# Token columns spread into rows: transposes of a repeated column in place of products with a unit or triangular matrix

## The reference, cut to what matters

```python
def rms_norm(x, g):
    xf = x.astype(F32)
    y = xf * lax.rsqrt(jnp.mean(xf * xf, axis=-1, keepdims=True) + EPS)
    return (y * g.astype(F32)).astype(x.dtype)
...
    # gated_delta_rule
    gc = jnp.cumsum(_chunk_gate(g), axis=-1)
    bc = _chunk_gate(beta)
    decay = jnp.exp(jnp.where(incl, gc[..., :, None] - gc[..., None, :], -jnp.inf))
...
    # mlstm_chunkwise, step
        d_log = jnp.where(incl, b_i[..., :, None] - b_i[..., None, :] + i_i[..., None, :], -jnp.inf)
        m_inter = b_i + m[..., None]
        m_t = jnp.maximum(m_inter, jnp.max(d_log, axis=-1))
        s = jnp.einsum('bhcd,bhsd->bhcs', q_i, k_i) * jnp.exp(d_log - m_t[..., None])
        den = w_inter * jnp.einsum('bhcd,bhd->bhc', q_i, n_bar) + jnp.sum(s, axis=-1)
        h = num / jnp.maximum(jnp.abs(den), jnp.exp(-m_t))[..., None]
```

## Time and profile before

| | |
|---|---|
| median of 3 runs | 2105.59 us (2104.49 to 2108.33) |
| the profiled execution | 2102.33 us, its span 2100.5 us |
| TensorE busy | 1995.4 us (95%), stationary loads 1251.3 us (60%) |
| VectorE, ScalarE, GpSimd busy | 716.2, 543.8, 120.3 us |
| the chain that ended last | PE 75%, DMA 19%, DVE 3% |
| mean granted TensorE clock | 0.978 |

### The profile page before, as it was taken

One profiled execution on the slowest core, in us unless ns is written; L12 is line 12 of the kernel. 1 busy time (PEld: TensorE's weight loads), 2 busy tenths in 40 slices (PEclk: granted clock), 3 DMA queues, 4 the chain that ended last, 5 costly groups with the idle time before them and its releaser, 6 DMA issues.

```text
span 2100.5 us, 22631 instructions
## 1 busy us (share of the span) xinstructions
PE 1995.4 (95%) x9262; PEld 1251.3 (60%) x9262; DVE 716.2 (34%) x1025; ACT 543.8 (26%) x831; POOL 120.3 (6%) x127
## 2 busy tenths in 40 slices
PE   8999999989898998989899899999999999999998
PEld 6868843333233333333233388898878888887886
DVE  6747321101010010101010275733568544335324
ACT  5246310001010100000010255234444333234125
POOL 3431000000000000000000000141000000000000
PEclk9998999999999999999999999999999999999999
DMA  9421799999999999999999822111113222223231
GB/s 266 142 71 48 298 354 425 427 427 427 428 428 429 429 428 428 428 428 429 429 427 427 339 109 81 61 41 41 61 58 140 83 94 87 84 115 110 100 141 61
DMA packets 48742, 516.27 MB, mean 246 GB/s; under 512 B 5904, under 2 KB 6032, under 8 KB 13088
## 3 DMA queue, kind: packets, MB, share of 16 engines
q1 hardware_dynamic: 46496, 508.39, 59.5%
q0 software_dynamic: 2176, 6.88, 1.5%
HBM read 508.92 MB, written 6.29 MB: 245 GB/s over the span
## 4 chain that ended last, share of the span: by engine, by line
PE 75%; DMA 19%; DVE 3%; ACT 1%; issue 1%; SPq 0%; POOL 0%; DVEq 0%; ACTq 0%
DMA arena<-in_w_gu_dram 19%; PE bank L2422 15%; PE bank L2447 5%; PE bank L912 4%; PE bank L910 4%; PE bank L911 4%; PE bank L576 3%; PE bank L578 3%; PE bank L577 3%; PE bank L2385 3%; PE bank L942 2%; PE bank L943 2%; PE bank L944 2%; PE bank L2050 2%; PE bank L2056 2%; PE bank L2052 2%
## 5 line engine op out<-in xcount | busy, mean ns | idle before, releaser
L2422 PE MATMUL bank<-arena 128*64 128x512 f32 x2048 | 480.6, 625 | 70.9 <-DMA arena<-in_w_gu_dram 67.0
L2422 PEld LDWEIGHTS bank<-arena 128*64 128x64 f32 x2048 | 162.4, 143 | 364.2 <-issue 357.6
L2917 DVE TENSOR_TENSOR arena<-arena,bank 128x256 f32<-128x256 f32 x64 | 26.9, 421 | 643.0 <-ACT arena L3158 643.0
L2447 PE MATMUL bank<-arena 128*64 128x512 f32 x1024 | 232.5, 595 | 0.6 <-ACT arena L3162 0.6
L3158 ACT ACTIVATE arena<-bank 128x256 f32<-128x256 f32 x64 | 24.6, 384 | 539.5 <-PE bank L2422 539.5
L2447 PEld LDWEIGHTS bank<-arena 128*64 128x64 f32 x1024 | 73.5, 137 | 139.4 <-issue 139.4
L910 PE MATMUL bank<-input_rounded,weight_rest 128*128 128x512 f32 x352 | 137.1, 390 | 0.0
L912 PE MATMUL bank<-input_rounded,weight_rounded 128*128 128x512 f32 x352 | 136.9, 389 | 0.0
L911 PE MATMUL bank<-input_rest,weight_rounded 128*128 128x512 f32 x352 | 136.9, 389 | 0.0
L576 PE MATMUL bank<-input_rounded,weight_rest 128*128 128x512 f32 x312 | 126.0, 404 | 0.0
L578 PE MATMUL bank<-input_rounded,unit_rounded 128*128 128x512 f32 x312 | 122.3, 392 | 0.0
(11 more groups left out here) (523 smaller groups left out, 2949.3 us busy)
## 6 DMA issues: line engine op xcount, KB each, us to landing
arena<-in_w_gu_dram SPq DMA_DIRECT2D x126, 2048.0 KB, 26.9
arena<-in_w_d_dram SPq DMA_DIRECT2D x62, 2048.0 KB, 26.8
arena<-in_wpack_dram SPq DMA_DIRECT2D x83, 1024.0 KB, 4.9
arena<-in_w_d_dram SPq DMA_DIRECT2D x4, 1024.0 KB, 9.5
arena<-in_w_gu_dram SPq DMA_DIRECT2D x3, 1024.0 KB, 7.3
arena<-in_xT_dram SPq DMA_DIRECT2D x4, 512.0 KB, 7.3
arena<-in_x_dram SPq DMA_DIRECT2D x2, 1024.0 KB, 12.9
arena<-in_x_dram SPq DMA_DIRECT2D x1, 2048.0 KB, 8.3
```

What stands on the lines that cost most here:

```text
L2422: last = mm(ab[64 * x:64 * x + 64, :], xsT[:, k, 64 * x:64 * x + 64], w[x][k], start=k == 0, stop=k == KD - 1)
L2447: last = mm(bank[4 + n][64 * x:64 * x + 64, :], hidT[c % 2][:, P * t + 64 * x:P * t + 64 * x + 64], w[:, x, t, 512 * n:512 * n + 512], sta ...
```

## The change

Thirteen groups of four products outside the mLSTM heads become groups of four transposes of the same repeated column: L645, L682 and L684 in four rounds, L920, L2090, and L2216 twice. L682 now takes the finished running sums `gc`, since a transpose adds nothing up. In the heads the 4-row product L801 goes, and four transposes of the maximum's columns take its place, behind the score products of L805. The columns are made by four more small transposes of `mxrow` and copied by VectorE together with `acol` (one copy of 32 columns, ahead of the gate unit's scaling and no longer behind it); ScalarE's exponential for `emcol` waits for that copy, and TensorE's first gate unit for `em_made`.

```diff
--- before.py
+++ after.py
@@ -357,7 +357,8 @@
         ebg = view(GS + 352, NT, 4)
         edec = view(GS + 368, NT, 4)
         ea = view(GS + 384, 4)
-        acol = view(GS + 388, NT, 4)
+        amcol = view(GS + 64, 32)
+        acol, mxcol = view(GS + 64, NT, 4), view(GS + 80, NT, 4)
         emcol = view(GS + 404, NT, 4)
         gsm = view(GS + 420, 64)
         T0 = B + 20480
@@ -642,7 +643,7 @@
             unit_products(2, bank[2][:, :])
             pe.wait_ge(S("r_made"), 1)
             for i in range(NT):
-                last = mm(bank[7][:, P * i:P * i + P], r13[:, i:i + 1].to_broadcast([P, P]), ident, start=True, stop=True)
+                last = turn(bank[7][:, P * i:P * i + P], r13[:, i:i + 1].to_broadcast([P, P]), ident)
             last.then_inc(S("rrow_filled"), 1)
             unit_products(3, bank[3][:, :])
             unit_products(U_GATES, bank[5][:, :])
@@ -679,9 +680,9 @@
                 if n == 0:
                     pe.wait_ge(S("mv_copied"), NT)
                 for h in range(4):
-                    mm(hv(bank[0], h), gg[:, n, h:h + 1].to_broadcast([P, P]), utri, start=True, stop=True)
+                    turn(hv(bank[0], h), gc[:, n, h:h + 1].to_broadcast([P, P]), ident)
                 for h in range(4):
-                    last = mm(hv(bank[1], h), beta2[:, n, h:h + 1].to_broadcast([P, P]), ident, start=True, stop=True)
+                    last = turn(hv(bank[1], h), beta2[:, n, h:h + 1].to_broadcast([P, P]), ident)
                 last.then_inc(S("gb_filled"), 1)
                 for h in range(4):
                     mm(hv(bank[2], h), qkv[:, 4 + h, t], qkv[:, h, t], start=True, stop=True)
@@ -790,7 +791,8 @@
             pe.wait_ge(S("mrow_made"), nth("mrow_made", 1))
             for i in range(NT):
                 turn(bank[2][:, 4 * i:4 * i + 4], arow[0:4, P * i:P * i + P], ident[0:4, 0:4])
-                last = turn(bank[2][:, 16 + 4 * i:20 + 4 * i], mrow[0:4, P * i:P * i + P], ident[0:4, 0:4])
+                turn(bank[2][:, 16 + 4 * i:20 + 4 * i], mxrow[0:4, P * i:P * i + P], ident[0:4, 0:4])
+                last = turn(bank[2][:, 32 + 4 * i:36 + 4 * i], mrow[0:4, P * i:P * i + P], ident[0:4, 0:4])
             last.then_inc(S("mcol_filled"), 1)
             pe.wait_ge(S("mv_one"), 1)
             pe.wait_ge(S("sg_scaled"), 4)
@@ -798,15 +800,18 @@
 
                 if h:
                     pe.wait_ge(S("mp_made"), h)
-                mm(bank[3][:, :], ident[0:4, h:h + 1].to_broadcast([4, P]), mxrow[0:4, :], start=True, stop=True)\
-                    .then_inc(S("mb_filled"), 1)
                 q = slice(MQ * (h % 2), MQ * (h % 2) + MQ)
                 for a, (b, o) in enumerate(((4, 0), (5, 0), (6, 0), (5, 384))):
                     last = mm(bank[b][:, o:o + L - P * a], mk[q, h // 2, P * a:P * a + P], mq[q, h // 2, P * a:L],
                               start=True, stop=True)
                 last.then_inc(S("ms_filled"), 1)
                 if h == 0:
-                    pe.wait_ge(S("mx_made"), 1)
+                    pe.wait_ge(S("mcol_copied"), 1)
+                for i in range(NT):
+                    last = turn(bank[3][:, P * i:P * i + P], mxcol[:, i, h:h + 1].to_broadcast([P, P]), ident)
+                last.then_inc(S("mb_filled"), 1)
+                if h == 0:
+                    pe.wait_ge(S("em_made"), nth("em_made", 1))
                 gate_half(5 + 2 * h, 0)
                 gate_half(5 + 2 * h, 1)
                 pe.wait_ge(S("mp_made"), h + 1)
@@ -917,7 +922,7 @@
             up_tile(C_UP, 1, 0, 1, first=True)
             pe.wait_ge(S("r_made"), 2)
             for i in range(NT):
-                last = mm(bank[4][:, P * i:P * i + P], nstat[N4][:, i:i + 1].to_broadcast([P, P]), ident, start=True, stop=True)
+                last = turn(bank[4][:, P * i:P * i + P], nstat[N4][:, i:i + 1].to_broadcast([P, P]), ident)
             last.then_inc(S("rrow_filled"), 1)
             for q in range(1, 4):
                 up_tile(C_UP + 2 * (q // 2), 2 * (q // 2) + 1, q % 2, q + 1)
@@ -1223,11 +1228,10 @@
                                        op0=ALU.max, op1=ALU.bypass))
             own.wait()
             tt(out=mrow[0:4, :], in0=brow[0:4, :], in1=mxrow[0:4, :], op=ALU.add).then_inc(S("mrow_made"), 1)
+            dve.wait_ge(S("mcol_filled"), nth("mcol_filled", 1))
+            dve.tensor_copy(amcol, bank[2][:, 0:32]).then_inc(S("mcol_copied"), 1)
             gate_scale(4)
-            dve.wait_ge(S("mcol_filled"), nth("mcol_filled", 1))
-            dve.wait_ge(S("em_made"), nth("em_made", 1))
-            own(dve.tensor_copy(acol.rearrange("p i h -> p (i h)"), bank[2][:, 0:16]))
-            own.wait()
+            dve.wait_ge(S("mcol_copied"), 1)
             offs = (0, 512, 896, 1152)
             where = ((4, 0), (5, 0), (6, 0), (5, 384))
             for h in range(MH):
@@ -1253,6 +1257,8 @@
                 dve.engine_nop().then_inc(S("mp_made"), 1)
                 gate_scale(5 + 2 * h)
                 dve.wait_ge(S("mo_filled"), nth("mo_filled", h + 1))
+                if h == 0:
+                    dve.wait_ge(S("em_made"), nth("em_made", 1))
                 for i in range(NT):
                     o = 129 * (i % 2)
                     dn = den[:, i:i + 1]
@@ -1611,8 +1617,8 @@
                 if n == 1:
                     fn(moT, moT, ACT.Sigmoid).then_inc(S("head_gates2"), 1)
             gate_out(4)
-            act.wait_ge(S("mcol_filled"), nth("mcol_filled", 1))
-            fn(emcol.rearrange("p i h -> p (i h)"), bank[2][:, 16:32], ACT.Exp, scale=-1.0).then_inc(S("em_made"), 1)
+            act.wait_ge(S("mcol_copied"), 1)
+            fn(emcol.rearrange("p i h -> p (i h)"), bank[2][:, 32:48], ACT.Exp, scale=-1.0).then_inc(S("em_made"), 1)
 
             def head_squares(br):
                 if br:
@@ -2087,7 +2093,7 @@
             pe.wait_ge(S("consts_in"), 16)
             pe.wait_ge(S("r1_made"), 1)
             for i in range(NT):
-                last = mm(bank[0][:, P * i:P * i + P], r1[:, i:i + 1].to_broadcast([P, P]), ident, start=True, stop=True)
+                last = turn(bank[0][:, P * i:P * i + P], r1[:, i:i + 1].to_broadcast([P, P]), ident)
             last.then_inc(S("sq1_summed"), 1)
             proj(3)
             pe.wait_ge(S("fnet_in"), 16 * 5)
@@ -2213,7 +2219,7 @@
             def channel_rows(n, q):
                 pe.wait_ge(S("hr_made"), n)
                 for i in range(NT):
-                    last = mm(bank[4][:, P * i:P * i + P], hr[q][:, i:i + 1].to_broadcast([P, P]), ident, start=True, stop=True)
+                    last = turn(bank[4][:, P * i:P * i + P], hr[q][:, i:i + 1].to_broadcast([P, P]), ident)
                 last.then_inc(S("hrow_filled"), 1)
 
             def mixed_product(c, i, ks):
```

## The result

The changed kernel takes **2112.71 us** (median of 10 runs, 2110.92 to 2116.43) against 2105.01 us (10 runs, 2102.33 to 2108.33) for the kernel before on the same chip: a ratio of **1.0040, 95% interval 1.0031 to 1.0049**, slower by some 8 us. The prediction was 2111.1 us, slower.

What follows compares the result with a forecast made beforehand. TensorE, busy 95% of the span, was taken as the bound. Heads' cost 4.93 us less 2.78 saved gave +2.15, plus 3.4 for half clock: +5.55 us, 2111.1 us against the median; range 2105.5 to 2114.5.

Steps and rivals of the forecast that it cites:

- The price of a group: TensorE, each spread: four transposes leave 0.44 us where four fp32 products leave 0.90, so 0.45 us saved; bounds 0 and 0.45.
- The channel rows, L2216: Two groups in the first layer's channel rows: 0.28 us gained at the first, 0.45 at the second, 0.73 together.
- The delta rule: Eight groups in four rounds: only VectorE's fourth-round wait for L684 counts, 0.70 us saved, not 3.6; bounds 0.2 and 1.6.
- The wait ahead of L709 and the clock there: Behind the delta rule's rounds: wait grows from 0.48 to about 2.5 us; half clock 0 to 1.7 us, taken as 0.
- The heads, waiting: Four mLSTM heads: spread behind L805 fills later, so L817 moves later; cost 0.3 + 1.84 + 0.95 + 1.84 = 4.93 us.
- The heads, clock: Ahead of L817: two of three longer waits end in half clock at 1.7 us each, +3.4 us; bounds 0 and 5.1.
- The base: Whole kernel: profiled execution took 2102.33 us, 3.3 below the median of 2105.59, to which the forecast sum is added.
- The sum: Whole kernel: 2.15 + 3.4 = +5.55 us, 2111.1 us against the median.
- That the clock holds at the three waits: Rival, heads ahead of L817: no half clock follows, so +2.15 us, 2107.7 us; chance 0.23.
- Hidden cover: Rival, heads: unseen cover behind the spread lets L817 keep its distance less 0.61 us; -4.6 us, 2101.0 us; chance 0.08.
- Transposes of a repeated column no cheaper: Rival, all spreads: the 2.78 us saving falls away, heads cost 1.3 more; 2111.8, up to 2116 us; chance 0.07.
- Transposes that don't hold the clock up: Rival, heads, delta rule's rounds and third wait: half clock follows transposes, some 6.8 us more, 2114.5 us; chance 0.05.

Runs made afterwards that it cites:

- fourth_round_products: spread_first with the delta rule's two groups of the fourth round as fp32 products again; 2099.59 us, ratio 0.9980.
- cover_wait: The changed kernel with twelve products of the next gate unit ahead of L822 in place of behind it; 2100.09 us, ratio 0.9982.
- product_behind: The kernel before with L801, still a product, moved behind L805 in all four heads; 2115.01 us, ratio 1.0053.
- spread_first: The changed kernel with the maximum's four transposes ahead of the score products in heads two to four; 2100.29 us, ratio 0.9977.
- heads_only: The kernel before with the mLSTM part of the change alone; 2114.59 us, ratio 1.0042.

## Why the prediction was right, step by step

- **The price of a group.** Said 0.45 us. From L2096 to the next work 0.35 us, for 0.80 before: right, and L920's group gave 0.43 to 0.45. The Trainium skill, page "TensorE: Matmul & The Clock Gate", section "Terms", has the transpose mode four times faster for fp32, which would be 0.60 us here and 0.67 by the pace of the earlier trace rows; the trace disagrees, it is a factor of about two.
- **The channel rows, L2216.** Said 0.28 + 0.45. Not told apart: one execution of the changed kernel had a stretch at half clock of 10.2 us there and was 1.27 us late at 333 us, the second had 6.8 us and was 0.46 us early. The means of the table give a hint: at 333 us the eight traces with these transposes and L2096's stand 1.4 us ahead of the five without, where 0.45 + 0.73 = 1.2 was said, and at 1173 us, behind the experts, still 0.9. Traces of one side differ by 2 to 3.2 us, so it stays a hint.
- **The delta rule.** Said 0.70, measured 0.80, but **the step put it in the wrong round**. I read VectorE's wait of 0.70 us for L684 as the fourth round's own. fourth_round_products kept the gain with products in that round. Before the change TensorE waits once in the rounds, ahead of the second, and goes on to the fourth without waiting; with the change it waits for VectorE ahead of the fourth too:

```profile
1326.14 1.16 PE L682 MATMUL bank<-arena 128*128 128x128 f32 x8 [0.75 <-DVEq L1149]
```

```profile
1350.48 0.65 PE L683 MATMUL bank<-arena 128*128 128x128 f32 x4 [0.18 <-DVEq L1154]
```

So TensorE was late in the fourth round by the sum of what stood in the last three, and the 1.8 us saved in the second and the third do there what the fourth's own 0.9 was said to do. With all three it saves 2.7 us, far more than VectorE uses: 0.8 is VectorE's gain, 0.18 the wait ahead of the fourth round, and 1.6 appears as the longer wait ahead of L709. "What TensorE saves in the others turns into waiting" holds for the first round alone.
- **The wait ahead of L709 and the clock there: mis-sized.** Said a wait of about 2.5 us, and its clock taken as 0 of 0 to 1.7. The wait is 2.1, and 6.8 us at half clock followed in six of the seven traces that have it; there the kernels lost 1.4 to 2.2 us (changed 1.82 in both). Of the six traces with 0.5 or 1.1 us three show 3.4 us at half clock and lose 1.4. In the mean 1.49 against 0.68 us, so by these 13 executions the longer wait costs some 0.8 us. That was not isolated, and cover_wait's two profiles show that the wait alone doesn't decide.
- **The heads, waiting.** Said 0.3 + 1.84 + 0.95 + 1.84 = 4.93. Measured from the first small transpose to the second head's start 1520.11 - 1502.26 = 17.85 us for 1517.96 - 1500.72 = 17.24, 0.61; the second head 1539.59 - 1520.11 = 19.48 for 17.59, 1.89; from head's start to L822 in the third 11.57 for 10.58, 0.99, in the fourth 11.57 for 9.70, 1.87. Sum 5.36. The step held: L1242 was said to start 3.00 us behind the head's start and L822 11.53, and they start at 3.04 and 11.57. That it is the place, and not the transposes, product_behind and spread_first show. In the first head the cost of 0.3, a choice between 0 and 0.74, was half of the 0.61 measured.
- **The heads, clock.** Said two of three stretches at 1.7, 3.4. Two of three it was, but the fourth head's is 6.8 us long: from L822's start to L835 it took 1582.62 - 1572.01 = 10.61 us for 7.82, 2.8 us; in the third, from L822's start to the next head, 1560.44 - 1551.16 = 9.28 for 1553.90 - 1546.13 = 7.77, 1.5. Sum 4.3, and with the 5.36 of waiting it makes the 9.7 of the table. That two of three waits were followed by half clock was a choice and came out by luck in part: the same heads in heads_only have 6.8 and 3.4 us in the other order, and no row said which. The mis-sized term is the length of a stretch: I had priced one that the shortest row showed, and its longest row, 9.37 - 7.09 = 2.3, would have been nearer.
- **The base.** The traces put the changed kernel 8.7 to 10.8 us behind before, the medians 7.7. Both profiled executions of before (2100.5 and 2102.2 us) are shorter than its median less the 1.8 us around the span, 2103.2. Neither has the half clock near 1365 us that two other kernels with its waits show; how often a run of it has, no run here tells. The first has its stretch in the third head besides, which costs 0.8 us less than one in the first.
- **The sum.** Said +5.55 us, measured +7.7 (2112.71 - 2105.01). Three terms were too small: the waiting in the heads by 0.43, their clock by 0.9 and the clock behind L709, taken as 0, by up to 1.8, some 3.1 together. The place of the first profile's stretch gives 0.8 of that back, and the median of before, 2105.59 when the prediction was made and 2105.01 over ten runs, another 0.6. The mechanism held; that 2111.1 lies only 1.6 us from the result is luck by these two.

**The rivals.** That the clock holds at the three waits (2107.7): excluded by the stretches at 0.50 in the third and the fourth head, in both profiles. Hidden cover (faster): L822 came at 11.57 us, not 9.7, so no. Transposes of a repeated column no cheaper: excluded by the rows of L2096. Transposes that don't hold the clock up: in spread_first and cover_wait the clock is 1.00 through four heads with four large transposes each behind or ahead of the score products. The Trainium skill, the same page, section "Part 4: PE-mode transpose", says that transposes don't count as busy for the clock gate; the windows at 1.00 speak against a cost from it in the heads. They don't test it where transposes stand alone. The one such place is L708, sixteen transposes with waits between them, which the change doesn't touch: half clock stands there or right behind in nine of the thirteen traces and in four it doesn't, so there the rule is neither excluded nor shown.

## What to carry to other kernels

An instruction that another engine waits for is worth its place in the queue, not its own length: the cheaper spread (0.44 us for 1.05) lost 8 us behind 2.35 us of score products that nobody was waiting for yet, and gained 2 to 3 us in its old place (the heads in the table; 5 with the 13 other groups, by the medians). Before moving such a producer, follow the path from it to the instruction where its engine waits again, and see how much slack stands there; here TensorE's wait of 0.52 us ahead of L817 said that there was none. Where the place can't be had, fill the wait with work that stands behind it: twelve products moved by one line brought all of it back, and the clock with it.

## What the runs showed that I had not expected

- Half clock is not a property of the kernel alone. Three kernels were profiled twice: before had 3.4 us at 0.50 at 1539 us once and at 1505 us the other time, and cover_wait none or 6.8 us near 1362, with the waits ahead of these places equal to 0.1 us. A term for it is a chance, worth 1.4 to 2.2 us near 1362 where it fell at all and 0.8 by where it fell in the heads, and a single profile can't price it.
- The stretches behind the 3.1 us waits of the heads repeated within 0.5 us in both profiles of the changed kernel, while the 3.1 us wait of the second head was followed by none in both. But heads_only, with the same waits in its heads, has the longer stretch in the third head and the shorter in the fourth, so the waits alone don't decide it.
- In the first head five of the six traces with the 4-row product have 3.4 us at half clock from 1505 us on, and none of the seven with transposes has. The prediction has no term for it. What in the change does so was not isolated: it alters the waits of the first head as well as its instructions.
- Saved busy time of 8 x 0.45 = 3.6 us on the engine that is busy 95% of the span brought 0.8 us in the delta rule, all of it as VectorE's wait in the fourth round.
